# Three decoder blocks in float32 pairs: all 42 halves of the gate/up products by seven products, and who makes their weight sums and low halves

## Time and profile before

| | |
|---|---|
| time, median of 3 | 1713.11 us (1712.53 to 1713.64) |
| the profiled execution | 1712.91 us, its span 1711.1 us |
| TensorE busy | 1700.8 us (99%), 9596 matmuls |
| VectorE | 1278.1 us (75%) |
| ScalarE | 864.3 us (51%) |
| GpSimd | 361.6 us (21%) |
| granted clock of TensorE | 0.999 |
| transfer queues | 152.9 MB, 89 GB/s over the span |

### The profile page before, as it was taken

The page is one execution under the profiler, slowest core; times in us unless marked ns, Lnnn a source line. Parts: engine busy times, 40 slices in busy tenths (PEclk is TensorE's granted clock), DMA queues, the critical chain, the costliest instruction groups (busy, mean ns, idle before and its releaser), DMA issues.

```text
span 1711.1 us, 24883 instructions
## 1 busy us (share of the span) xinstructions
PE 1700.8 (99%) x9596; PEld 1476.2 (86%) x9596; DVE 1278.1 (75%) x1968; ACT 864.3 (51%) x1530; POOL 361.6 (21%) x264
## 2 busy tenths in 40 slices
PE   9999999999999999999999999999999999999998
PEld 8888888998998888888888988889898888898897
DVE  5789656897696846695979966755889687996575
ACT  5554533443354646554545533547877454454354
POOL 2003204442325011102144202022110213520200
PEclk9999999999999999999999999999999999999999
DMA  5212333334222221213233341323111234334122
GB/s 173 74 62 72 99 99 124 99 99 146 77 75 87 62 82 57 73 51 98 88 134 111 99 123 50 90 74 93 40 50 50 87 95 127 99 99 136 62 87 74
DMA packets 125196, 152.90 MB, mean 89 GB/s; under 512 B 7526, under 2 KB 96904, under 8 KB 125080
## 3 DMA queue, kind: packets, MB, share of 16 engines
q1 hardware_dynamic: 124776, 150.99, 27.9%
q10 hardware_dynamic: 304, 0.33, 0.1%
HBM read 148.61 MB, written 2.10 MB: 88 GB/s over the span
## 4 chain that ended last, share of the span: by engine, by line
PE 94%; DVE 4%; POOL 1%; issue 1%; ACT 1%; DVEq 0%; ACTq 0%; POOLq 0%
PE bk L2422 23%; PE bk L2424 23%; PE bk L2423 23%; PE bk L2464 5%; PE bk L2466 5%; PE bk L2465 5%; PE bk L2427 4%; PE bk L2569 2%; DVE FS L2624 1%; POOL FS L3011 1%; PE bk L2603 1%; PE bk L2530 1%; PE bk L2602 1%; DVE WL L2636 1%; PE bk L2557 1%
## 5 line engine op out<-in xcount | busy, mean ns | idle before, releaser
L2422 PE MATMUL bk<-R,WH 128*128 128x512 f32 (+1 forms) x1394 | 521.2, 374 | 0.9 <-DVE WL L2636 0.7
L2424 PE MATMUL bk<-R,WL 128*128 128x512 f32 (+1 forms) x1394 | 515.0, 369 | 0.0
L2423 PE MATMUL bk<-R,WH 128*128 128x512 f32 (+1 forms) x1394 | 514.8, 369 | 0.0
L2636 DVE TENSOR_TENSOR WL<-RAW,WH 128x1024 fp32r<-128x1024 f32 (+5 forms) x198 | 248.2, 1255 | 153.5 <-ACT WH L2861 152.3
L2861 ACT ACTIVATE WH<-RAW 128x1024 fp32r<-128x1024 f32 (+5 forms) x198 | 202.8, 1026 | 213.8 <-PE bk L2424 152.5
L2422 PEld LDWEIGHTS bk<-R,WH 128*128 128x128 f32 x1394 | 263.0, 189 | 45.3 <-DVE WL L2636 2.1
L2424 PEld LDWEIGHTS bk<-R,WL 128*128 128x128 f32 x1394 | 262.8, 189 | 44.9
L2423 PEld LDWEIGHTS bk<-R,WH 128*128 128x128 f32 x1394 | 263.2, 189 | 41.0
L3007 POOL TENSOR_TENSOR OVER<-TOK 128x1024 f32<-128x1024 f32 x28 | 76.3, 2725 | 382.0 <-DVE WL L2633 216.4
L2464 PE MATMUL bk<-WH,R 128*128 128x512 f32 (+4 forms) x394 | 144.7, 367 | 0.0
L2466 PE MATMUL bk<-WL,R 128*128 128x512 f32 (+4 forms) x394 | 139.3, 353 | 0.0
(11 more groups left out here) (235 smaller groups left out, 3251.8 us busy)
## 6 DMA issues: line engine op xcount, KB each, us to landing
RAW<-in_ffn_w_down_dram SPq DMA_DIRECT2D x44, 512.0 KB, 3.9
RAW<-in_ffn_w_up_dram SPq DMA_DIRECT2D x64, 256.0 KB, 3.0
TOK<-in_ffn_w_up_dram SPq DMA_DIRECT2D x14, 1024.0 KB, 5.1
RAW<-in_ffn_w_up_dram SPq DMA_DIRECT2D x28, 512.0 KB, 3.6
RAW<-in_w_down_dram SPq DMA_DIRECT2D x22, 512.0 KB, 3.6
RAW<-in_da_w_qkv_dram SPq DMA_DIRECT2D x32, 256.0 KB, 3.0
TOK<-in_w_gate_dram SPq DMA_DIRECT2D x7, 1024.0 KB, 5.4
TOK<-in_w_up_dram SPq DMA_DIRECT2D x7, 1024.0 KB, 5.0
```

Source lines behind the costliest of these rows:

```text
L2422: e.matmul(dst, lh, rh, start=start, stop=False)
L2423: e.matmul(dst, lh, rl, start=False, stop=False)
L2424: return e.matmul(dst, ll, rh, start=False, stop=stop)
L2636: e.tensor_tensor(low, sides(st.n, raw_home(st.n)), high.bitcast(F32), ALU.subtract).then_inc(on["wlo_dve"], 1)
```

## The change

All 14 units more: in both conv layers the up half of blocks 4 to 10 becomes a unit too. The sums of weight blocks are steps `vsum` on VectorE. In the conv layers, the low halves of chunks 0 and 1 of each unit are made in another way: ScalarE writes the negated copy (`wneg`), and a DMA that GpSimd issues adds the raw block to it in place (`wadd`). A unit's load goes in two DMAs, one for each 128 columns, and lands in another layout. Results are joined in four VectorE instructions (three of 512 elements, one of 256) and two ScalarE copies; two pairs of products share a bank. In `Combined`, the makers wait for each other, have another rank, take two slots FS instead of four (the sums go to PART) and wait for a stated margin of free slots. The planner's costs are adapted.

```diff
-PARTS = (range(0, 4), range(4, 8), range(8, 11))
-SEVENS = ({fb: (0, 2) for fb in range(4, 11)}, {fb: (0,) for fb in range(4, 11)}, {fb: (0,) for fb in range(4, 11)})
+THIRDS = (range(0, 4), range(4, 8), range(8, 11))
+BLOCKS = (THIRDS, THIRDS, THIRDS)
+SEVENS = ({fb: (0, 2) for fb in range(4, 11)}, {fb: (0, 2) for fb in range(4, 11)}, {fb: (0, 2) for fb in range(4, 11)})
...
+EARLY = -2
+MARGIN = (3, 5, 5)
+RANKS = (1.5, 0.5)
+ADDED = ((),(0,1),(0,1))
+NADD = 4
+ON_V = (True, True)
...
+                if kind == "wadd":
+                    free_at[eng] = begins(eng, fields["after"]) + 900.0
+                    ready_at[id(fields["done"][0]), fields["done"][1]] = free_at[eng] + 3800.0
+                    continue
...
-        UNIT = [t[:, 0:2048].rearrange("p (k q c) -> p q k c", q=4, c=P) for t in FLAT]
+        UNIT = [t[:, 0:2048].rearrange("p (h k o c) -> p h o k c", h=2, o=2, c=P) for t in FLAT]
...
-            two = raw[:, 1:2].to_broadcast([P, 2, 4, P])
+            b11, b12 = raw[:, 0, 0], raw[:, 1, 0:1]
+            one = bass.AP(b11.tensor, b11.offset, [b11.ap[0], [9 * P, 2], [2 * P, 4], [1, P]])
+            two = b12.to_broadcast([P, 2, 4, P])
...
-            st = yield step("wsum", dst=SUMS[:, 0:2], x=raw[:, 0:4:3], y=two, after=counts([unit_in[u], sums_free[0]]))
-            unit_sums[u] = [st.pool]
+            kinds = ["vsum" if on_v else "wsum" for on_v in ON_V]
+            st = yield step(kinds[0], dst=SUMS[:, 0:2], x=one, y=two, after=counts([unit_in[u], sums_free[0]]))
+            done = st.dve if ON_V[0] else st.pool
+            unit_sums[u] = [done]
...
-                lo = w_low[n] = yield step("wlo", n=n, m=chunks[n][0] * chunks[n][1], after=[st.act])
+                if n in sevens and sevens[n][1] in ADDED[layer_of(n)]:
+                    k = adds[0]
+                    adds[0] += 1
+                    done = s_add[k % NADD], 16 * (k // NADD + 1)
+                    st = yield step("wneg", n=n, m=chunks[n][0] * chunks[n][1], after=[st.act])
+                    lo = yield step("wadd", n=n, done=done, after=[st.act, (done[0], done[1] - 16)] if k >= NADD else [st.act])
+                    lo.dve = done
+                    w_low[n] = lo
+                else:
+                    lo = w_low[n] = yield step("wlo", n=n, m=chunks[n][0] * chunks[n][1], after=[st.act])
...
-                        unit_comes(u + 2, [unit_sums[u], lo.dve])
+                        unit_comes(u + 2, [unit_sums[u], w_low[units[u][1][0]].dve, lo.dve])
...
-                for kp in range(4):
-                    spawn(self.make(kp), 0.5)
+                N.uses += 4
+                self.makers = [spawn(self.make(kp), RANKS[0]) for kp in range(4)]
...
-                while kp and self.own[kp - 1] is None:
+                while kp and (self.own[kp - 1] is None or ("s4", kp - 1) not in self.of):
...
-                while len(fsl.fr) < 5:
+                while len(fsl.fr) < self.margin:
                     yield None
-                e, o, p, q = slots = [fsl.get() for _ in range(4)]
-                E, O, A, B = (FS[:, s.i, 0:S] for s in slots)
+                e, o = fsl.get(), fsl.get()
+                E, O = (FS[:, s.i, 0:S] for s in (e, o))
+                A, B = PART
...
             def middle():
+                while q.first is None or len(fsl.fr) < 2:
+                    yield None
+                l, r = sorted((fsl.get(), fsl.get()), key=lambda s: s.i)
+                right = FS[:, r.i, 0:S]
+                st = yield step("join", dst=FS[:, l.i:r.i + 1:r.i - l.i, 0:256], src=halves_of(b2), x=one.unsqueeze(1).to_broadcast([P, 2, 256]),
+                                op=ALU.add, after=counts([done6, q.first, l.free, r.free]))
+                put_bank(b2, st.dve)
+                part_free[u % 2] = [st.dve]
+                third = yield step("join", dst=right[:, 256:S], src=BK[b7.i][:, 0:256], x=right[:, 0:256], op=ALU.add, after=counts([done7, st.dve]))
+                put_bank(b7, third.dve)
+                copied = yield step("keep", dst=FS[:, l.i, 256:S], src=right[:, 256:S], after=counts([third.dve, l.free]))
+                st = yield step("join", dst=right.rearrange("p (x c) -> p x c", x=2), src=BK[b5.i][:, 0:256].unsqueeze(1).to_broadcast([P, 2, 256]),
+                                x=right.rearrange("p (x c) -> p x c", x=2), op=ALU.subtract, after=counts([done5, third.dve, copied.act]))
...
-                    dst = FLAT[st.u % 2][:, 0:2048].rearrange("p (k c) -> p k c", c=256)
-                    e.dma_start(dst, units[st.u][0]).then_inc(s_unit[st.u % 2], 16)
+                    for h in (0, 1):
+                        dst = FLAT[st.u % 2][:, h * 1024:h * 1024 + 1024].rearrange("p (k c) -> p k c", c=P)
+                        e.dma_start(dst, units[st.u][0][:, :, h * P:h * P + P]).then_inc(s_unit[st.u % 2], 16)
...
+                elif k == "wneg":
+                    for done in st.after:
+                        w.wait_ge(*done)
+                    e.activation(four(st.n, home(st.n)[1]), of_unit(st.n), ACT.Copy, scale=-1.0).then_inc(on["wneg_act"], 1)
...
+                elif k == "wadd":
+                    for done in st.after:
+                        w.wait_ge(*done)
+                    u, q = sevens[st.n]
+                    raw = OVER[:, 2 * S * (q - 1):2 * S * q] if q else FLAT[u % 2][:, 0:SLOT]
+                    e.dma_start(home(st.n)[1], raw, accum_op=ALU.add).then_inc(st.done[0], 16)
```

More of the change, by code:

```diff
@@ L502, in plan_ffn @@
                 zones[layer] = [len(chunks), len(chunks), len(units)]
-            for fb in PARTS[part]:
+            parts = BLOCKS[layer]
+            for fb in parts[part]:
                 sevenfold = SEVENS[layer].get(fb, ())
@@ L1700, in seven @@
             q = Group()
-            q.first = q.second = q.third = q.left = q.right = q.y = None
-            one, two = PART[u % 2][:, 0:256], PART[u % 2][:, 256:S]
+            q.first = q.low = q.both = None
+            one = PART[u % 2][:, 0:256]
             def split(n):
@@ L1708, in split, with product @@
                 return w_low[n].dve
-            def product(n, half, name):
-                b = yield from bank("gemm")
-                st = yield step("piece", n=n, half=half, xs=X.operand(name), bank=b.i, after=counts([w_low[n].dve, X.ready, b.free]))
+            def product(n, half, name, b=None, o=0):
+                if b is None:
+                    b = yield from bank("gemm")
+                st = yield step("piece", n=n, half=half, xs=X.operand(name), bank=b.i, o=o, after=counts([w_low[n].dve, X.ready, b.free]))
                 if half or n == n2:
@@ L1746, in seven @@
             yield from split(n4)
[L1747 removed]
+            _, done6 = yield from product(n4, 0, "s2", b2, 256)
             def middle():
[L1750 removed]
+                while q.first is None or len(fsl.fr) < 2:
                     yield None
[L1752 to L1762 removed]
@@ L1764, in seven @@
-            spawn(middle(), 0)
-            b, done = yield from product(n4, 1, "a22")
-            def bottom_left(b, done):
-                while q.right is None:
-                    yield None
-                low = yield from join(FS[:, q.left.i, 256:S], b, done, one, ALU.add, q.third)
-                put_bank(b, low)
-                part_free[u % 2] = [low]
-                yield from ev(0, q.left, low)
-            spawn(bottom_left(b, done), 0)
-            yield from split(n2)
-            b, done = yield from product(n2, 0, "s4")
@@ new lines, in middle, with outer @@
+                put_bank(b5, st.dve)
+                q.low, q.both = [copied.act, st.dve], (l, r)
+            spawn(middle(), 0)
+            b4, _ = yield from product(n4, 1, "a22")
+            yield from split(n2)
+            _, done3 = yield from product(n2, 0, "s4", b4, 256)
+            X.over(done3)
+            def outer():
+                while q.both is None:
+                    yield None
+                l, r = q.both
+                at_l = FS[:, l.i, 256:S]
+                both = bass.AP(at_l.tensor, at_l.offset, [at_l.ap[0], [FW * (r.i - l.i) - 256, 2], [1, 256]])
+                st = yield step("join", dst=both, src=halves_of(b4), x=both, op=ALU.add, after=counts([done3, q.low]))
+                put_bank(b4, st.dve)
+                spawn(ev(0, l, st.dve), 0)
+                spawn(ev(1, r, st.dve), 0)
```

158 lines of the change are left out of this document (79 added, 79 removed).

## The result

| | median us | lowest to highest | runs | profiled run | its span |
|---|---|---|---|---|---|
| before | 1712.88 | 1712.53 to 1713.64 | 4 | 1712.9 | 1711.1 |
| after | 1727.22 | 1726.62 to 1728.26 | 4 | 1726.6 | 1724.8 |

The ratio is 1.0083, with an interval of 1.0071 to 1.0096: the change made the kernel slower by 14 us. The forecast was 1704.2 us, with 1701 to 1723 as its range. It was wrong in its sign, and the time lies outside the range.

A forecast was written before the change was run, and what follows sets the result against it. The prediction took TensorE's issue time to bound the kernel: 1713.1 us, less 10.9 for the new units, plus 2 for VectorE's lag, with adding transfers and prologue at nothing, gave 1704.2 us; range 1701 to 1723.

The forecast's parts named there:

- Part 1: Second halves of blocks 2 and 3: 14 ordinary halves become units, each 0.78 us cheaper on TensorE, saving 10.9 us.
- Part 2: VectorE's load: 19.4 us per step in the first block, 20.2 in the conv layers, beside 20.26 of TensorE.
- The 2 us for its lag: Cost taken for VectorE falling behind in the conv layers' four runs, within bounds of 0 and 14 us.
- Part 3: Adding transfers in the conv layers: 5.1 us each from issue to landing, adding nothing to the time.
- cycle: Loop through chunk 1's sums' buffer: two copies, transfer, next sum; 8.4 us, 9.6 with one queued instruction, under 10.13.
- the cover: Spare time of the chunk 1 loop against a unit's 10.13 us: 0.5 to 1.7 us.
- Rival A: Adding transfers late in the conv layers: at 6.8 us each, 24 units pay 29 us, giving 1731 us; chance 0.20.
- Part 4: Prologue's serial makers of operand sums fit beside the down projection: cost 0, bounds -0.4 to +5 us per layer.
- Rival C: Prologue operands late by 3 us in each layer, giving 1713 us; chance 0.08.
- B: VectorE bounds the conv layers, costing 7 to 10 us in place of 2, giving 1710 us; chance 0.17.

The follow-up runs named there:

- mix_36: Changed kernel with 36 units: in the conv layers both halves of blocks 4, 6, 8, 10, only the gate half of 5, 7, 9; 1705.36 us.
- mix_38: Changed kernel with 38 units: in the conv layers both halves of blocks 4, 6, 7, 8, 10, only the gate half of 5 and 9; 1703.55 us.
- units_28: Changed kernel with the 28 units of before, the conv layers' up halves ordinary again, all else of the change kept; 1711.56 us.
- before_42: Kernel before with all 42 units and nothing else changed: sums on GpSimd, every low half on VectorE; 1768.93 us.
- taps_quarter: Changed kernel, same instructions and order, each VectorE filter tap covering 128 of 512 tokens; 1721.00 us.
- plan_late: Changed kernel whose planner takes an adding transfer's landing to be 2 us later, so only the instruction order changes; 1743.72 us.
- adds_12: Changed kernel with the adding transfers on chunks 1 and 2 instead of 0 and 1; 1830.11 us.
- add_quarter: Changed kernel, same order, each adding transfer moving only 256 of its 1024 columns; 1714.48 us.
- load_quarter: Changed kernel with the conv layers' unit loads, except the first two of each layer, cut to a quarter of their rows; 1720.19 us.

## Why the prediction was wrong, by its steps

**Part 1 was right.** 0.78 us per half is what mix_36 and mix_38 gave, 6.2 us for 8 halves and 8.0 for 10 (from units_28). The first block's run took 80.63 us for 81. 41.7 us separate before_42 from the whole change, so the 14 units weren't to be had by themselves.

**Part 2 was right in its plain durations.** The blocks by GpSimd's sums are gone. The subtraction, which had taken up to 3.46 us, takes

```profile
L2673 DVE TENSOR_TENSOR WL<-OVER,WH x31: 1208/1219/1227, 310.6 to 1673.0; 128x1024 fp32r<-128x1024 f32 x31
```

and VectorE isn't the bound. The 2 us for its lag were on the wrong term: a wait of TensorE for its joins never appears. But a VectorE needed for 20.2 of 20.26 us had a queue of 6 us in front of a sum (from 961.6 to 967.52), and that queue belongs to Part 3's cycle. GpSimd fell by 118.7 us, not 160: the issues of 56 adding transfers, 56 x 0.86 = 48 us, were forgotten there. (3 MB in 10.13 us are 311 GB/s, not 312; nothing hangs on it.)

**Part 3 is the step that failed: "So nothing is added, and the cover is 0.5 to 1.7 us".** The transfer's length in it held: the landing's median is 5.2 us (5.1 taken). The cycle did not. Where VectorE wrote the next sum as soon as the transfer had landed, it was 964.32 - 955.14 = 9.2 us, within the 8.4 to 9.6 worked out. But the issues of chunk 1 through that run of eight, from 906.84 to 993.62 us, are 13.9, 11.2, 9.9, 13.3, 9.2, 15.3 and 14.0 us apart, over the 10.13 us of a unit in all but two. Rival A had its 1731 us from 6.8 us per transfer and "decides from about 6.5 us on"; by its own terms the limit is 6.8 us with nothing queued and 5.6 with one instruction. Its number was near by luck, for its mechanism was another one: at 5.2 us it should not have decided. What the prediction did wrong is that it priced each chunk by itself:

- The cycle doesn't end with chunk 1's sum. The other two sums follow on VectorE, with up to 6 us of other work between them, not one instruction, and ScalarE's fixed order puts chunk 0 of a later unit behind their copies. The late buffer delays a chunk that never goes through it. taps_quarter (-6.2 us), plan_late (+16.5 us) and adds_12 (+103 us) show that the queue, the order and the buffer each count; how they act together in front of the long wait is read from its timeline. Each unit falls back a little, so only the 5th and the 7th of a run are late: 38 units in runs of at most four lose nothing, the wait is 0.9 to 1.1 us in a run of six and 7.4 to 8.0 in one of eight.
- The transfers were taken at their median. The one on the late path met the unit's own load and took 8.4 us. "Unit load and adding transfer at the same time" wasn't in the sum at all; a quarter of the load saves 7.0 us, a quarter of the adding transfer 12.7, both 19.9.
- A wait of 6 us was priced at its length. It also costs 2.1 to 2.7 us at the lower clock afterwards.

The terms of the loss, each taken to a quarter: 19.9 us for the two transfers, 2.6 more for the taps on top of them (6.2 alone). 1704.72 us is left, against 1713.1 - 10.9 = 1702.2. The two waits of 2.4 us for chunk 1 in that run's trace are nearly all of these 2.5 us. That they come from ScalarE, whose copies no run made shorter, is argued only: its busy time is 20.61 of 25 us where the runs of eight begin. That stays open, and so does how much of the 6 us queue a hand-set place for the two sums would take away; it wasn't tried.

**Part 4 was right**: units_28, which has the whole new prologue, is not over the kernel before (1711.56 us against 1713.44). Rival C fell with it, and B too in its stated form: VectorE's joins aren't waited for, and its queue counts only inside the loop.

The prediction's own test, "wrong if runs of the second and third block take over 86 us", said what happened (91.9 and 91.1 us: 81 + 8.0 or 7.4 + the clock), and its sign for A, "TensorE waiting for a transfer", pointed at the right row.

## What to carry to other kernels

Where a transfer is put into a path that ends in a single buffer's reuse, write the whole loop down: the landing, the next write with the whole queue of its in-order engine in front of it, the copies behind it, and every independent instruction that stands behind these in a fixed order. Price the landing beside the kernel's own loads at that moment, not at its median. A nearly full VectorE did no harm on its own (24.38 of 25 us in the first block); inside such a loop, cutting its taps to a quarter saved 6.2 us. Where a loop has no slack, a little of the old work between the new units, 0.78 us dearer each, buys it back: 38 units in runs of at most four beat 42.

## What the runs showed of the hardware

- TensorE's granted clock fell to 0.50, the lower of its two levels, in its idle time of 6.4 us, and was back at 0.95 to 1.00 about 6 us after TensorE had resumed. After 3.5 us of idling it was 0.56 and then 0.76 for the next 2.5 us each (add_quarter), after 1.63 us it stayed at 1.00. The length of the idle time alone doesn't give the loss: behind a wait of 2.7 us in load_quarter the clock was 0.50 and then 0.82. The rows of add_quarter and of the changed kernel:

```profile
979.50:982.00 2.50, 2.29 (x11) 2.30 (x12) 2.50 (x5) 0.97 (x2) 0.00 (x0) 0.56 0.31 44
982.00:984.50 2.50, 2.50 (x18) 2.50 (x18) 2.24 (x4) 1.87 (x4) 0.00 (x0) 0.76 0.00 0
```

```profile
957.50:960.00 2.50, 2.50 (x22) 2.50 (x22) 1.29 (x3) 0.96 (x3) 0.00 (x0) 1.00 0.95 185
```

- An adding transfer of 512 KB from SBUF to SBUF takes 5.2 us from issue to landing. The queue's row of the page (packets, MB, share of the 16 engines) gives 0.088 x 1724.8 / 56 = 2.7 us of all engines for each. At 128 KB it lands after 2.7 us:

```profile
q0 software_dynamic: 8064, 29.36, 8.8%
```

- GpSimd's issue of it took 850 to 992 ns, with medians of 862 to 869, beside a VectorE that is busy up to 95%, mostly with instructions that read two tensors. No issue came near the 4.67 us that one of GpSimd's own operations had taken. That agrees with the Trainium skill, "SBUF — State Buffer", section "Who interferes with whom", which expects for such instructions that writing descriptors isn't stalled, and calls its reason inferred.
